# One decoder layer with a grouped mixture of experts: the final combine moved into the expert blocks

## The chip, the cores and the metric

The program runs on one NeuronCore of a Trainium2 chip. The metric is the device time of one execution in microseconds (us). Five engines work side by side, each through its own instructions in order: PE (TensorE, matmuls), DVE (VectorE), ACT (ScalarE), POOL (GpSimd) and SP (SyncE, which only issues DMAs). They meet at semaphores: an instruction raises one when it is done, and another engine waits for a value of it. A DMA raises its semaphore by 16 when it has landed.

## The reference, cut to what matters

The input is a residual stream x of 2048 tokens by 1024, in float32. One layer is computed: a recurrent token mixer, then a mixture of experts, then a last RMS norm.

```python
x = x + g1 * mixer(modulate(rmsnorm(x, norm1_g), sh1, sc1))
hn = modulate(rmsnorm(x, norm2_g), sh2, sc2)
# router: softmax over 16 experts in 4 groups of 4; the best group is chosen,
# and in it the two best experts, with gates that sum to 1
out = sum over the two experts e: (silu(hn @ w_gate[e]) * (hn @ w_up[e]) * gate[e]) @ w_down[e]
x = x + g2 * out
return rmsnorm(x, final_norm_g)
```

The kernel computes each token only for its two experts. Both are of the same group, which the change relies on.

## The kernel before, in words

The stages follow each other, each a block with a barrier behind it: `norm_and_transpose` and `lru` (the mixer), `out_and_norm` (the mixer's output product, the residual sum x2, the second norm and the router's logits), `dispatch`, `experts` and `combine`.

**Tiles.** A token tile has 128 tokens (one per partition); there are NT = 16. `out_and_norm` keeps the 16 tiles of x2 in SBUF for the rest of the program and writes the normed rows hn2 to DRAM.

**Dispatch.** Every (token, expert) pair gets a slot. Slots are sorted by expert, and each expert's slots are filled up to full blocks of 128; at most MAXB = 48 blocks, of which 39 are used with these inputs. Tables in SBUF hold, for each block, the expert, the token of each slot (`slot_token`), the gate of each slot (`slot_gate`), and where weights have to be prepared (`split0`, `split1`). `tab["pos"]` holds for each token its two slots. DVE works these tables out; SP meanwhile fills the unused blocks of the slot buffer `yslot` in DRAM (10 stores, L995).

**Experts.** Products are done in three passes, with each operand as a high and a low part (`w_hi`, `w_lo`, `e_xh`, `e_xl`, `e_ah`, `e_al`). For block b the steps are:

- POOL, `gather(b)`: copies the block's column of token numbers (L1226) and starts an indirect DMA of 128 rows of hn2 into `xg` (L1229). There is one `xg`, so it waits until PE has turned the block before.
- PE, `turn(b)`: transposes `xg`. ACT `high_x`, DVE `low_x`: copy and subtract. PE, `gate_up(b)`: 24 matmuls. ACT `tanh`, DVE `act_product`; PE `turn_act(b)` inside the next block's `gate_up`; ACT `high_a`, DVE `low_a`; PE `down(b)`: 12 matmuls into `pd`.
- DVE, `y_scaled(b)`: `ysb = pd * slot_gate * g2row` (L1327). ACT, `store(b)`: writes `ysb` to its block of yslot (L1277). There is one `ysb`, so the next `y_scaled` waits until the store has landed.

In one turn of its loop each engine works on different blocks: PE does gate_up(i+2), turn(i+3), down(i+1); DVE low_a(i+1), act_product(i+2), low_x(i+3), y_scaled(i+1), low_w(i+2); POOL gather(i+3), low_w(i+1). The order within an engine is as written.

**Weights.** The weights of an expert are four quarters of 128x1536. SP loads them into two raw buffers (quarters 0 and 2, 1 and 3); ACT `high_w` copies a quarter to `w_hi` (L1272); `low_w` subtracts it for `w_lo` (L1214), DVE the even ones and POOL the odd ones. The next expert's quarters 0 and 1 are made in the first block of an expert, 2 and 3 in its second; if it has one block alone, all in that. In further blocks there are none. `low_w` reads per block from the tables whether a piece is due, and if so expert and buffer, into registers.

**Combine.** For each of the 16 token tiles POOL gathers the rows of the token's two slots from yslot (L1446 index copy, L1451 two indirect DMAs), DVE adds them (L1483), adds them to x2 (L1485), ACT squares and sums (L1473) and takes the root (L1475), DVE takes the reciprocal (L1489) and scales by it and by the gain (L1493), SP stores the output tile. Four buffers.

## Time and profile before

| | us |
|---|---|
| three runs: median (lowest to highest) | 1336.73 (1335.91 to 1336.91) |
| the profiled execution | 1335.74 |
| its span, first to last instruction | 1334.2 |
| PE, DVE, ACT, POOL busy | 1082.2, 769.5, 567.3, 563.5 |
| moved by DMA | 207.59 MB, mean 156 GB/s |

The span is the time between the first and the last instruction of the profiled execution; its own time is a little longer. Busy time is the sum of the durations of an engine's instructions, without waits and without the issue of DMAs by other engines than POOL. A share over the whole span is a mean over stages with different limits, so the rows further down are cut by stage.

### The profile page before, as it was taken

Reading aid. Unit: us, or ns where it says so; the run is one execution under the profiler, and the core shown is the slowest. Engines: PE = TensorE matmul, PEld = TensorE weight load, DVE = VectorE, ACT = ScalarE, POOL = GpSimd, SP = SyncE. Lnnn points to the kernel's source line nnn. Section 1 sums busy time; section 2 is a strip of 40 time slices with the busy share of each in tenths; the row PEclk is TensorE's granted clock in tenths of the full one; section 3 lists DMA queues with packets and bytes.
Section 4 is the critical chain, followed back from the end, with each engine's and each line's share of the span. In section 5 each row is a group of like instructions: output and inputs, shape, how many; then the busy total and the mean of one; then the engine's idle time right before and its main releaser. Section 6 shows DMA issues by size and latency. Waiting matters only on the chain. (4 is left out here: it accounts for less than half of the span.)

```text
span 1334.2 us, 19676 instructions
## 1 busy us (share of the span) xinstructions
PE 1082.2 (81%) x4894; PEld 866.6 (65%) x4895; DVE 769.5 (58%) x874; ACT 567.3 (43%) x792; POOL 563.5 (42%) x394
## 2 busy tenths in 40 slices
PE   1459999999999994899999814899999999989300
PEld 0247778778778773688888714677777776767200
DVE  6984676667667664545343376354544545445288
ACT  1554666766776673422222220333433334334033
POOL 0686625525526420145455243333433333334273
PEclk9999999999999997899999855999999999999755
DMA  8544314313313201833324144466756567667498
GB/s 303 175 89 151 99 33 130 84 46 114 93 53 114 63 16 38 311 126 98 139 94 141 48 142 174 135 210 209 262 199 228 189 211 241 206 207 236 145 350 324
DMA packets 126572, 207.59 MB, mean 156 GB/s; under 512 B 16961, under 2 KB 84545, under 8 KB 126417
## 3 DMA queue, kind: packets, MB, share of 16 engines
q1 hardware_dynamic: 106096, 132.81, 30.7%
q0 software_dynamic: 14832, 54.01, 12.0%
q10 hardware_dynamic: 5616, 20.45, 3.8%
q8 instruction: 12, 0.20, 0.1%
q14 instruction: 16, 0.12, 0.0%
HBM read 156.36 MB, written 50.87 MB: 155 GB/s over the span
## 5 line engine op out<-in xcount | busy, mean ns | idle before, releaser
L1214 POOL TENSOR_TENSOR w_lo<-w_raw,w_hi 128x1536 f32 x30 | 107.1, 3570 | 157.8 <-ACT w_hi L1272 157.8
L1377 PE MATMUL e_gu<-w_hi,e_xh 128*128 x312 | 130.2, 417 | 13.7 <-issue 5.0
L1272 ACT ACTIVATE w_hi<-w_raw 128x1536 f32 x60 | 88.3, 1486 | 121.1 <-PE e_pd L1402 46.3
L849 PE MATMUL po<-wo_hi,b_yh 128*128 128x512 f32 x256 | 102.9, 402 | 25.6 <-DVE wo_lo L779 25.6
L1379 PE MATMUL e_gu<-w_hi,e_xl 128*128 x312 | 123.5, 396 | 0.0
L1378 PE MATMUL e_gu<-w_lo,e_xh 128*128 x312 | 122.8, 394 | 0.0
L823 POOL TENSOR_TENSOR x<-x,b_xr 128x1024 f32 (+1 forms) x15 | 49.1, 3273 | 171.9 <-DVE x L787 171.9
L531 DVE SCALAR_TENSOR_TENSOR XB<-xu,conv_w,XB 128x512 f32<-128x512 f32 x96 | 92.6, 965 | 42.2 <-ACT XB L401 38.5
L624 PE MATMUL px<-hT_hi,wx_hi 128*128 128x512 f32 x256 | 101.7, 397 | 5.1 <-DVE wx_lo L465 5.1
L624 PE MATMUL pg<-hT_hi,wg_hi 128*128 128x512 f32 x256 | 104.2, 407 | 0.0
L625 PE MATMUL px<-hT_lo,wx_hi 128*128 128x512 f32 x256 | 101.6, 397 | 0.0
L626 PE MATMUL px<-hT_hi,wx_lo 128*128 128x512 f32 x256 | 101.4, 396 | 0.0
L626 PE MATMUL pg<-hT_hi,wg_lo 128*128 128x512 f32 x256 | 101.1, 395 | 0.0
L625 PE MATMUL pg<-hT_lo,wg_hi 128*128 128x512 f32 x256 | 101.1, 395 | 0.0
L850 PE MATMUL po<-wo_lo,b_yh 128*128 128x512 f32 x256 | 100.4, 392 | 0.0
L851 PE MATMUL po<-wo_hi,b_yl 128*128 128x512 f32 x256 | 100.4, 392 | 0.0
L1327 DVE SCALAR_TENSOR_TENSOR e_y<-e_pd,t_slot_gate,g2row 128x1024 f32<-128x1024 f32 x39 | 50.1, 1284 | 66.2 <-DMA yslot_scratch<-e_y 37.8
L606 POOL TENSOR_TENSOR macc<-macc,mtmp 128x512 f32<-128x512 f32 x56 | 84.4, 1507 | 4.7
L1377 PEld LDWEIGHTS e_gu<-w_hi,e_xh 128*128 128x128 f32 x312 | 59.3, 190 | 39.7 <-issue 29.9
L787 DVE TENSOR_TENSOR x<-po,g1row 128x1024 f32 (+1 forms) x16 | 19.6, 1224 | 108.7 <-PE po L851 108.7
L600 POOL TENSOR_SCALAR macc<-stg,cond 128x512 f32<-128x512 f32 x8 | 12.1, 1512 | 155.2 <-PE pmod L647 151.3
L1400 PE MATMUL e_pd<-w_hi,e_ah 128*128 x156 | 64.8, 415 | 12.1 <-issue 6.5
(260 smaller groups left out, 2639.4 us busy)
## 6 DMA issues: line engine op xcount, KB each, us to landing
yslot_scratch<-e_y ACTq DMA_DIRECT2D x39, 512.0 KB
stg<-in_ada_w_dram POOLq DMA_DIRECT2D x32, 512.0 KB, 4.2
w_raw<-in_moe_w_gate_dram SPq DMA_DIRECT2D x32, 384.0 KB, 3.3
w_raw<-in_moe_w_up_dram SPq DMA_DIRECT2D x32, 384.0 KB, 4.0
n_ada<-in_ada_w_dram SPq DMA_DIRECT2D x16, 512.0 KB, 4.8
n_x<-in_x_dram SPq DMA_DIRECT2D x16, 512.0 KB, 3.4
y_scratch<-M SPq DMA_DIRECT2D x16, 512.0 KB, 3.0
b_yt<-y_scratch SPq DMA_DIRECT2D x16, 512.0 KB, 5.3
```

The costliest lines, as they stand in the source:

```text
L531: nc.vector.scalar_tensor_tensor(xb, xu[:, n, w:w + NB], cw[:, ds(j, 1), w], xb, ALU.mult, ALU.add).then_inc(done, 1)
L624: nc.tensor.matmul(dst[:], whi[br][:, k], hT_hi[:, k, cols], start=(k == 0), stop=False)
L625: nc.tensor.matmul(dst[:], whi[br][:, k], hT_lo[:, k, cols], start=False, stop=False)
L626: last = nc.tensor.matmul(dst[:], wlo[br][:, k], hT_hi[:, k, cols], start=False, stop=(k == KD - 1))
L849: nc.tensor.matmul(po[u][:, cols], yh[u][:, tok], wo_hi[:, k, cols], start=(k == 0), stop=False)
L850: nc.tensor.matmul(po[u][:, cols], yh[u][:, tok], wo_lo[:, k, cols], start=False, stop=False)
L851: last = nc.tensor.matmul(po[u][:, cols], yl[u][:, tok], wo_hi[:, k, cols], start=False, stop=(k == KD - 1))
L1214: tensor_tensor(w["lo"][:, ds(off + q * QW, QW)], w["raw"][:, q % 2], w["hi"][:, ds(off + q * QW, QW)].bitcast(F32), ALU.subtract).then_in ...
L1272: nc.scalar.activation(w["hi"][:, ds(off + q * QW, QW)], w["raw"][:, q % 2], ACT.Copy).then_inc(w["hi_done"], 1)
L1377: nc.tensor.matmul(gu[:], xh[:, tok], hi, start=(k == 0), stop=False)
L1378: nc.tensor.matmul(gu[:], xh[:, tok], lo, start=False, stop=False)
L1379: last = nc.tensor.matmul(gu[:], xl[:, tok], hi, start=False, stop=(k == KD - 1))
```

## The change

The stage `combine`, the slot buffer yslot, its fills and the resident x2 go. Instead:

- `out_and_norm` stores each tile of x2 to DRAM (`x2_dram`), on SP, between the load and the store of hn2.
- Experts are processed in the order 0, 4, 8, 12, 1, 5, ... (`expert_at`): the first experts of the four groups, then the second ones, and so on. The two experts of a token lie at least four experts apart in that order. DVE writes the mask and the positions in this order; SP's loop over experts is written out.
- Each slot gets a code that says whether it is the token's first or second slot. DVE makes three tables of row numbers from it: `row` (the token), `row_first` (the token where the slot is its first, otherwise a number out of range) and `row_second` (likewise for the second). Indirect DMAs skip rows out of range.
- The gate is now multiplied in `act_product`. For each block, POOL gathers the rows of x2 into `xa` (`gather_x`); DVE adds `ysb` to them in `ab` (`accumulate`); POOL scatters `ab` back to x2_dram where it was the first slot (`scatter_acc`); ACT squares and sums `ab` (`square`); POOL works out the reciprocal root by a power and one Newton step, five instructions (`root`); DVE scales to `ob` (`normed`); POOL scatters `ob` to the output where it was the second slot (`scatter_out`). `ysb`, `xa`, `ab` and `ob` are single buffers.

The first and the last turns of the loops are written out in the same manner. The core of the diff:

```diff
-def out_and_norm(nc, sem, cst, io, x2, y_dram, mod_dram, hn2_dram, g2row, logits):
+def out_and_norm(nc, sem, cst, io, y_dram, mod_dram, hn2_dram, x2_dram, g2row, logits):
...
+            def store_x2(it, u):
+                sp.wait_ge(resid, it + 1)
...
+                if at_least(it, 2):
+                    sp.wait_ge(x2_stored[u], it * 8 - u * 8)
...
+                sp.dma_start(x2_dram[ds(it * P, P), :], x2[:, ds(it, 1)].rearrange("p o n -> p (o n)"))\
+                    .then_inc(x2_stored[u], 16)
...
-            pipelined(sp, NT, 6, [(load, 0), (store, 4)])
+            pipelined(sp, NT, 6, [(load, 0), (store_x2, 3), (store, 4)])
...
+def expert_at(i):
+
+    return i % G * PER + i // G
...
@@ dispatch
-            sp.wait_ge(ends_ready, 1)
...
-            with sp.Fori(used, MAXB + 1) as b:
-                sp.dma_start(yslot_dram[ds(b * P, P), :], g2row[:]).then_inc(filled, 16)
...
+            for c in range(TOPK):
+                done(v.tensor_tensor(later[:, c], posf[:, c], posf[:, 1 - c], ALU.is_gt))
+            v.scalar_tensor_tensor(tok2[:], later[:].rearrange("p c t -> p (c t)"), float(SECOND), tok2[:],
+                                   ALU.mult, ALU.add).then_inc(code_ready, 1)
...
-            done(v.tensor_copy(tab["slot_token"][:], pslot[:, 0:MAXB]))
+            done(v.tensor_copy(sci[:], pslot[:, 0:MAXB]))
+            done(v.tensor_scalar(skip1[:], sci[:], float(SECOND), None, ALU.is_gt))
+            done(v.scalar_tensor_tensor(sci[:], skip1[:], -float(SECOND), sci[:], ALU.mult, ALU.add))
+            done(v.tensor_scalar(skip2[:], sci[:], 0.0, float(SKIP), ALU.is_equal, ALU.mult))
+            done(v.tensor_scalar(sci[:], sci[:], -1.0, None, ALU.add))
+            done(v.tensor_tensor(sci[:], sci[:], skip2[:], ALU.add))
+            done(v.tensor_copy(tab["row"][:], sci[:]))
+            done(v.scalar_tensor_tensor(skip2[:], skip1[:], float(SKIP), sci[:], ALU.mult, ALU.add))
+            done(v.tensor_copy(tab["row_first"][:], skip2[:]))
+            done(v.tensor_scalar(skip1[:], skip1[:], -float(SKIP), float(SKIP), ALU.mult, ALU.add))
+            done(v.tensor_tensor(skip1[:], skip1[:], sci[:], ALU.add))
+            done(v.tensor_copy(tab["row_second"][:], skip1[:]))
...
@@ experts, POOL
+            def gather_x(b, first=False):
+                if not first:
+                    pool.wait_ge(xa_in, b * 16)
+                    pool.wait_ge(acc_ready, b)
...
+                nc.gpsimd.tensor_copy(idx_x[:], tab["row"][:, ds(b, 1)]).then_inc(idx_x_ready, 1)
+                pool.wait_ge(idx_x_ready, b + 1)
...
+                pool.indirect_dma_start(xa[:], None, x2_dram, rows(idx_x), **bound).then_inc(xa_in, 16)
+
+            def scatter_acc(b, first=False):
+                if not first:
+                    pool.wait_ge(acc_out, b * 16)
...
+                nc.gpsimd.tensor_copy(idx_a[:], tab["row_first"][:, ds(b, 1)]).then_inc(idx_a_ready, 1)
+                pool.wait_ge(idx_a_ready, b + 1)
+                pool.wait_ge(acc_ready, b + 1)
...
+                pool.indirect_dma_start(x2_dram, rows(idx_a), ab[:], None, **bound).then_inc(acc_out, 16)
+
+            def scatter_out(b, first=False):
+                if not first:
+                    pool.wait_ge(out_done, b * 16)
...
+                nc.gpsimd.tensor_copy(idx_o[:], tab["row_second"][:, ds(b, 1)]).then_inc(idx_o_ready, 1)
+                pool.wait_ge(idx_o_ready, b + 1)
+                pool.wait_ge(out_ready, b + 1)
...
+                pool.indirect_dma_start(out[0], rows(idx_o), ob[:], None, **bound).then_inc(out_done, 16)
+
+            def root(b, first=False):
+
+                pool.wait_ge(squared, b + 1)
...
+                nc.gpsimd.tensor_scalar(var[:], ssq[:], 1.0 / D, EPS, ALU.mult, ALU.add).then_inc(rstd_step, 1)
...
+                nc.gpsimd.tensor_tensor(root0[:], var[:], nhalf[:], ALU.pow).then_inc(rstd_step, 1)
...
+                nc.gpsimd.tensor_tensor(part[:], root0[:], root0[:], ALU.mult).then_inc(rstd_step, 1)
...
+                nc.gpsimd.tensor_scalar(part[:], part[:], var[:], -0.5, ALU.mult, ALU.mult).then_inc(rstd_step, 1)
...
+                if not first:
+                    pool.wait_ge(out_ready, b)
...
+                nc.gpsimd.tensor_scalar(rstd[:], part[:], 1.5, root0[:], ALU.add, ALU.mult).then_inc(rstd_ready, 1)
+
+            nc.gpsimd.memset(xg[:], 0.0).then_inc(cleared, 1)
+            nc.gpsimd.memset(xa[:], 0.0).then_inc(cleared, 1)
+            nc.gpsimd.memset(nhalf[:], -0.5).then_inc(cleared, 1)
...
-            with pool.Fori(0, nless) as i:
+            with pool.Fori(3, nless) as i:
                 gather(i + LEAD)
                 low_w(pool, nc.gpsimd.tensor_tensor, i + 1, 1)
+                scatter_acc(i - 1)
+                gather_x(i)
+                root(i - 1)
+                scatter_out(i - 2)
...
@@ experts, ACT
+            def square(b, first=False):
+                act.wait_ge(acc_ready, b + 1)
+                if not first:
+                    act.wait_ge(rstd_ready, b)
...
+                nc.scalar.activation(squares[:], ab[:], ACT.Square, accum_out=ssq[:]).then_inc(squared, 1)
...
+            with act.Fori(2, nless) as i:
+                square(i - 1)
                 high_a(i + 1)
                 tanh(i + 2)
-                store(i)
                 high_x(i + 3)
                 high_w(i + 2)
...
@@ experts, DVE
-                nc.vector.scalar_tensor_tensor(ysb[:], pd[:], tab["slot_gate"][:, ds(b, 1)], g2row[:],
-                                               ALU.mult, ALU.mult).then_inc(y_ready, 1)
+                nc.vector.tensor_tensor(ysb[:], pd[:], g2row[:], ALU.mult).then_inc(y_ready, 1)
+
+            def accumulate(b, first=False):
+                dve.wait_ge(y_ready, b + 1)
+                dve.wait_ge(xa_in, (b + 1) * 16)
+                if not first:
+                    dve.wait_ge(squared, b)
+                    dve.wait_ge(out_ready, b)
+                    dve.wait_ge(acc_out, b * 16)
+                nc.vector.tensor_tensor(ab[:], ysb[:], xa[:], ALU.add).then_inc(acc_ready, 1)
+
+            def normed(b, first=False):
+                dve.wait_ge(rstd_ready, b + 1)
+                if first:
+                    dve.wait_ge(fg_in, 16)
+                else:
+                    dve.wait_ge(out_done, b * 16)
...
+                nc.vector.scalar_tensor_tensor(ob[:], ab[:], rstd[:], fg[:], ALU.mult, ALU.mult).then_inc(out_ready, 1)
...
+            with dve.Fori(2, nless) as i:
                 low_a(i + 1)
                 act_product(i + 2)
                 low_x(i + 3)
                 dues = [per_block(dve, f"split{part}", i + 2, 0, 1) for part in range(2)]
+                normed(i - 1)
+                accumulate(i)
                 y_scaled(i + 1)
                 low_w(dve, nc.vector.tensor_tensor, i + 2, 0, dues)
...
-def combine(nc, sem, cst, io, tab, x2, yslot_dram, out):
...
```

## Rows read from the trace of the kernel before

**Rows 1.** Windows by stage; columns: five engines busy us (count), clock, DMA share, GB/s.

```profile
0.00:120.00 120.00, 57.20 (x204) 41.10 (x206) 91.82 (x113) 49.85 (x84) 66.75 (x38) 1.00 0.60 190
...
780.00:828.00 48.00, 17.60 (x68) 15.36 (x68) 40.83 (x78) 3.70 (x3) 24.31 (x21) 0.50 0.47 175
828.00:1252.00 424.00, 386.50 (x1794) 302.76 (x1794) 200.88 (x264) 157.45 (x216) 151.18 (x108) 0.98 0.61 203
1252.00:1334.00 82.00, 0.00 (x0) 0.00 (x0) 60.57 (x65) 24.40 (x49) 45.00 (x48) 0.51 0.85 320
```

**Rows 2.** The page's chain that ended last, by engine and line.

```profile
DVE f_ya L1483 1%; DVE x L1485 1%; DMA f_yb<-yslot_scratch,f_idx 1%; POOL f_yb L1451 0%; POOL f_ya L1451 0%; DVE f_ob L1493 0%; POOL f_idx L1446 0%; DVE f_rstd L1489 0%; ACT f_junk L1473 0%; DVEq L1485 0%; DVEq L1492 0%; DVEq L1484 0%; ACT f_std L1475 0%; DVEq L48 0%; DVEq L1493 0%
```

**Rows 3.** Groups by form, 800 to 1334 us: xcount, busy us, mean ns, idle.

```profile
L1493 DVE SCALAR_TENSOR_TENSOR f_ob<-x,f_rstd,f_g 128x1024 f32<-128x1024 f32 x16 | 20.5, 1284 | 2.1 <-DVE f_rstd L1489 0.8
L1483 DVE TENSOR_TENSOR f_ya<-f_ya,f_yb 128x1024 f32<-128x1024 f32 x16 | 19.6, 1222 | 14.2 <-DMA f_yb<-yslot_scratch,f_idx 14.2
```

**Rows 4.** Timeline of DVE: start us, length us, instruction, idle before.

```profile
856.76 1.28 DVE L1327 SCALAR_TENSOR_TENSOR e_y<-e_pd,t_slot_gate,g2row 128x1024 f32<-128x1024 f32 x1 [1.31 <-PE e_pd L1402]
...
1251.31 1.28 DVE L1327 SCALAR_TENSOR_TENSOR e_y<-e_pd,t_slot_gate,g2row 128x1024 f32<-128x1024 f32 x1 [3.45 <-PE e_pd L1402]
```

**Rows 5.** Waits of POOL, 828 to 1256 us; us in total, times, longest.

```profile
POOL w_lo L1214 <- ACT w_hi L1272: 157.8, 30, 9.0
POOL e_idx L1226 <- PE e_tp L1359: 66.2, 10, 7.8
```

**Rows 6.** Timeline of all engines where the expert stage starts.

```profile
826.28 0.21 DVE L1143 TENSOR_SCALAR t_slot_gate<-pslot 128x48 f32<-128x48 f32 x1
...
874.03 1.09 ACT L1253 ACTIVATE e_xh<-e_tp 128x512 fp32r<-128x512 f32 x2 [0.49 <-PE e_tp L1359]
...
880.61 3.79 POOL L1214 TENSOR_TENSOR w_lo<-w_raw,w_hi 128x1536 f32 x1 [4.46 <-ACT w_hi L1272]
```

**Rows 7.** Groups of POOL by form, whole span.

```profile
L951 POOL MEMSET keep<- 128x256 f32 x1 | 0.3, 313 | 0.0
```

**Rows 8.** Timeline of POOL at the start of the combine.

```profile
1261.19 0.94 POOL L1451 DMA_INDIRECT f_yb<-yslot_scratch,f_idx  x1 [0.30 <-issue]
1262.14 0.19 POOL L1446 COPY f_idx<-t_pos 128x2 int32<-128x2 int32 x1
1263.10 0.96 POOL L1451 DMA_INDIRECT f_ya<-yslot_scratch,f_idx  x1 [0.77 <-POOL f_idx L1446]
```

**Rows 9.** Groups by form, 828 to 1252 us.

```profile
L1214 POOL TENSOR_TENSOR w_lo<-w_raw,w_hi 128x1536 f32 x30 | 107.1, 3570 | 157.8 <-ACT w_hi L1272 157.8
```

**Rows 10.** Tile e_xg; durations ns min/median/max, and its landing.

```profile
L1229 POOL DMA_INDIRECT e_xg<-hn_scratch,e_idx x39: 961/983/1084, 828.9 to 1224.8; - x39
...
DMA to landing us min/median/max: 4.2/5.3/7.6
```

**Rows 11.** Timeline: ACT stores e_y, and the next e_y of DVE.

```profile
1190.30 0.34 ACTq L1277 DMA_DIRECT2D yslot_scratch<-e_y  x1
...
1193.96 1.28 DVE L1327 SCALAR_TENSOR_TENSOR e_y<-e_pd,t_slot_gate,g2row 128x1024 f32<-128x1024 f32 x1 [1.08 <-DMA yslot_scratch<-e_y]
```

**Rows 12.** Timeline of ACT before a weight copy.

```profile
1200.91 1.09 ACT L1253 ACTIVATE e_xh<-e_tp 128x512 fp32r<-128x512 f32 x2 [0.49 <-PE e_tp L1359]
1205.03 1.49 ACT L1272 ACTIVATE w_hi<-w_raw 128x1536 f32 x1 [3.03 <-issue]
```

**Rows 13.** Timeline of POOL later in the combine, DVE adding beside it.

```profile
1281.19 0.90 POOL L1446 COPY f_idx<-t_pos 128x2 int32 x1
1282.87 1.41 POOL L1451 DMA_INDIRECT f_ya<-yslot_scratch,f_idx  x1 [0.77 <-POOL f_idx L1446]
```

**Rows 14.** Timeline of POOL in the block with two pieces.

```profile
1179.56 3.68 POOL L1214 TENSOR_TENSOR w_lo<-w_raw,w_hi 128x1536 f32 x1 [4.18 <-ACT w_hi L1272]
1189.38 3.52 POOL L1214 TENSOR_TENSOR w_lo<-w_raw,w_hi 128x1536 f32 x1 [6.13 <-ACT w_hi L1272]
```

**Rows 15.** Windows around PE's longest stand in the expert stage.

```profile
1180.00:1185.00 5.00, 4.79 (x13) 3.38 (x14) 0.00 (x0) 0.31 (x1) 3.24 (x1) 0.66 0.61 181
```

More of the change, by code:

```diff
@@ L1161, in _, with experts @@
                                  start=(it == 0), stop=(it == N - 1)).then_inc(slotted, 1)
-def experts(nc, sem, cst, io, tab, w, hn2_dram, yslot_dram, g2row):
+def experts(nc, sem, cst, io, tab, w, hn2_dram, x2_dram, g2row, out):
     ctx = ExitStack()
@@ L1198, in _ @@
                 load_quarter(sp, io, w, 1, q)
-            with sp.Fori(2, E) as e:
+            sp.dma_start(fg[:], io["final_norm_g"].partition_broadcast(P)).then_inc(fg_in, 16)
+            for e in range(2, E):
                 for q in range(NQ):
@@ L1337, in _ @@
             low_w(dve, nc.vector.tensor_tensor, 1, 0)
-            with dve.Fori(0, nless) as i:
+            low_a(1)
+            act_product(2)
+            low_x(3)
+            accumulate(0, True)
+            y_scaled(1)
+            low_w(dve, nc.vector.tensor_tensor, 2, 0)
+            low_a(2)
+            act_product(3)
+            low_x(4)
+            normed(0, True)
+            accumulate(1)
+            y_scaled(2)
+            low_w(dve, nc.vector.tensor_tensor, 3, 0)
+            with dve.Fori(2, nless) as i:
                 low_a(i + 1)
@@ L1346, in _ @@
             act_product(nless + 2)
+            normed(nless - 1)
+            accumulate(nless)
             y_scaled(nless + 1)
@@ L1349, in _ @@
             low_a(nless + 2)
+            normed(nless)
+            accumulate(nless + 1)
             y_scaled(nless + 2)
+            normed(nless + 1)
+            accumulate(nless + 2, )
+            normed(nless + 2)
         @block.tensor
@@ L1541, in build @@
                  "hi_done": sem("w_hi_done"), "lo_done": [sem("w_lo_done0"), sem("w_lo_done1")]}
[L1542 to L1544 removed]
+            dispatch(nc, sem, cst, io, logits, tab, w)
+            experts(nc, sem, cst, io, tab, w, hn2_dram, x2_dram, g2row, out)
 _INS = ["x", "c", "ada_w", "ada_b", "norm1_g", "norm2_g", "lru_w_in", "lru_conv_w", "lru_conv_b", "lru_wa", "lru_ba",
```

220 lines of the change are left out of this document (110 added, 110 removed).

## The prediction

> **What bounds the kernel now.** I read the windows by stage first, then the chain of waits, then the waits of POOL. From 828 to 1252 us runs the expert stage: PE is busy for 386.5 of 424 us at a clock of 0.98, so PE bounds it, while POOL is busy for 151 us only. From 1252 to 1334 runs the combine: PE does nothing, DVE is busy for 60.6 of 82 us [rows 1]. The chain that ended last names the three large DVE operations of the combine and its gathers [rows 2]; two of them last 1.22 and 1.28 us [rows 3]. So 82 us can be won. What they are bought with is the period of the expert stage: the scaled outputs of blocks 0 and 38 start at 856.76 and 1251.31 [rows 4], 394.5 us for 38 blocks, 10.4 us each. There are 39 blocks. 29 of them carry weight splitting on POOL (30 pieces, two in one block); the other 10 don't. Before these pieces POOL waits 157.8 us for ACT, and 66.2 us for PE's turns in the 10 blocks without [rows 5]. POOL's 151 busy us hide its pauses, which matters below.
>
> **Start of the stage.** After the last product DVE does 13 small operations where it did 2, at 0.21 us like the last one there [rows 6]: +2.3. POOL clears two tiles of 128x1024 and a column before its first gather; a memset of a quarter of the size takes 0.31 [rows 7], so I take 2.3 for all (bounds 0.6 and 2.6). The stage starts 4.6 us later. The removed fills on SP, three removed casts, the stores of x2 in the stage before (16 of them on SP, waiting for a sum that is ready before the hn2 row that SP stores next) and the gain row on SP are taken at nothing: another engine's work ends each stage. They cost 2 us if that cover is gone.
>
> **POOL's work for one block.** Before: one indirect DMA. After: four (gather of hn2, gather of x2, scatter of the sum, scatter of the output), each with its own index copy, and five small operations for the root. In the combine a copy of 0.19 starts as soon as a DMA ends, a pause of 0.77 and the next DMA of 0.96 follow, and a second DMA comes 0.30 after a first [rows 8]: with the expert stage's 0.98 for the DMA [rows 10], 1.94 us per indirect transfer, and the engine does nothing else in the pause, since it runs in order. Four are 7.76. The root: five operations of 0.19 (the index copy's duration) and four handovers on the same engine. Below stand 0.08 (1.27 in all), above 0.47, which is the pause of 0.77 less the 0.30 that a DMA takes anyway (with a fifth, 3.3 in all); I take 0.2, so 1.75, as the pause is that of an instruction that DMA issue follows, not arithmetic. A weight piece is 3.5 [rows 9]. A block with a piece therefore holds POOL for 7.76 + 1.75 + 3.5 = 13.0 us, one without for 9.5. The first is already over the 10.4 of PE.
>
> **The loop across the engines.** The tiles ab, xa and ob are single. DVE's normed(b) waits until scatter_out(b-1) has landed; accumulate(b+1) stands behind it on DVE, and scatter_acc(b+1) waits for that; on POOL gather_x(b+2), root(b+1) and then scatter_out(b) follow, which the next normed waits for. One turn of this loop yields one block: normed 1.28 + 0.06, accumulate 1.22 [rows 3], handover 0.1; the scatter's DMA, whose index is already copied, 0.30 + 0.98; gather_x 1.94; root 1.75; copy and pause of scatter_out 0.96; its landing L; handover 0.1. For L the gathers show 4.2 at least and 5.3 as median [rows 10]; ACT's store to DRAM, issued at 1190.30, releases DVE at 1193.96, 3.7 later [rows 11]. A scatter whose rows out of range are skipped moves half the bytes, but stands behind gather_x in the same queue: I take 4.4, bounds 3.7 and 5.3. Sum 13.1 us (bounds 11.7 and 15.5). So even a block without a weight piece takes 13.1, and POOL's gather and piece lie in the landing.
>
> The Trainium skill (DMA: Bandwidth & Descriptors, "Anatomy of one DMA — SWDGE (gpsimd) path") fits a transfer by 2.0 us plus bytes over 436 GB/s. By it a 512 KB gather takes 3.2, and the trace disagrees (4.2 at least). With 2.6 for the half-filled scatter, the loop would be 11.3, the blocks with a piece would still be set by POOL's sum, and the time would be 18 us less.
>
> **What is added in a block with a piece.** Two costs have no row on POOL. First its register reads: with two branches and five reads ACT starts a weight copy 3.03 us after the end of the copies before it, for "issue" alone [rows 12]; POOL has three or four reads, and 0.98 of DMA to hide them, so 0 to 1.7. Second, POOL against DVE: while DVE adds tiles from SBUF in the combine, an index copy takes 0.90 for 0.20 and a DMA 1.41 for 0.96 [rows 13]. Normed and accumulate, 2.5 us of such work, fall into POOL's piece after the change: 0 to 1.6. I take 1.3 for both together: 14.3 us (bounds 12.5 and 17.7).
>
> The Trainium skill (GPSIMD Engine Reference, "Key points") says that the two engines share their SBUF interface and collide when a DVE instruction has two SBUF inputs. The trace agrees; taken to the full it gives the upper 1.6 in each of 26 such blocks, 42 us in all.
>
> **The sum.** Block 4 is turned at 874.03 [rows 6]; plus 4.6, 878.6. POOL: gather(5) to 880.6; the piece that began at 880.61 begins at 885.2 and ends at 888.9; scatter_acc(1), gather_x(2), root(1) and the copy of scatter_out(0) take 1.94 + 1.94 + 1.75 + 0.96, to 895.5; landing and handover to 900.0; normed(1) and accumulate(2) end at 902.6. From accumulate(2) to accumulate(38) are 36 periods. The pieces of blocks 4 to 38 lie in them: 27, as 3 came earlier. The split of tokens over experts is the same, only their order changes, so one block still has both: the second piece began 6.13 after the end of the first, waiting for the weights [rows 14], +6.1 + 3.5. That makes 25 x 14.3 = 357.5, one of 23.9, and 10 x 13.1 = 131: 512.4. After accumulate(38): square 1.3, root 1.75, normed 1.4, the last scatter 0.4 + 4.4: 9.3. Span 902.6 + 512.4 + 9.3 = 1424. The profiled execution took 1335.74 for a span of 1334.2, so 1.5 outside, and the median of the three runs lies 1.0 above it: **1427 us**, 6.7% slower. What the combine gives back (82) is over-paid by 36 periods of 14.2 on average instead of 10.4 (138); the later start, the first turns of the loop and the tail are the other 34. With the low bounds everywhere the periods are 25 x 12.5 + 22.1 + 10 x 11.7 = 451.6 and the time 1365; with the high ones 1543.
>
> **PE in all this** has 9.9 us of work in some 14. It will stand still for two spells a block, for its turn and for e_al, since ACT's square now comes ahead of high_a. Before, a stand of 4 us took the clock from 2.4 to 1.2 GHz for a while (0.66 over 5 us, so 1.7 us lost) [rows 15]. PE has over 3 us free per block to cover that. It is a term of its own only if the clock stays low throughout: see below.
>
> **Rivals.**
> 1. *It all hides under PE.* The period stays 10.4, the last e_y comes 4.6 later than now, and accumulate and the tail follow: 1251.31 + 4.6 + 1.3 + 1.2 + 9.3 + 2.5 = 1270 us, 5% faster. It needs POOL to hold under 10.4 on average with 0.77 x 3.5 = 2.7 for pieces: (10.4 - 2.7 - 1.3) / 4 = 1.6 us for each indirect transfer, against 1.94, and a loop of 10.4 against 11.7 at least. For it speaks only that POOL is busy for 151 of 424 us now. 5%.
> 2. *POOL bounds, the loop hides.* POOL's sum alone at its low price, 39 x (7.76 + 1.27) + 30 x 3.5 = 457, from 832.4, with 20 for the first turns and the last block's chain and 2.5 around: 1312, 1.8% faster. The point is whether normed finds scatter_out landed; the order on POOL (scatter_out last, right after root) speaks against. 5%; with partial waits it comes out within 0.2% of now, 3%.
> 3. *The clock stays at 1.2 GHz.* PE's 9.9 us become nearly 20, 39 x 9 more than 10.4: some 1640 us. In the first 120 us PE stood still half of the time at full clock [rows 1], which speaks against; from 780 to 828, at 17.6 busy of 48, it ran at 0.50, which speaks for. 3%.
> 4. *My forecast*, 84%, with its upper end (registers, collisions and long landings together, over 1480) at 7 of these; its own range is 1350 to 1480.
>
> **Chances and range.** A measurement of this kernel tells 0.2% (2.7 us) from no change. Faster: rivals 1 and 2, 0.10. Same 0.03. Slower 0.87. I leave out the two faster cases, the slow clock and the top, 0.20 in all, and reach down to no change: 1334 to 1480.
>
> **What the profile after would show.** Right: PE busy for about two thirds of the stage; DVE's longest wait is that of e_ob for the DMA out<-e_ob; POOL with few waits in blocks with a piece; e_ab 13 us apart without a piece, 14 to 15 with; about 1.9 us from index copy to end of each DMA; last e_ab near 1415. Wrong: if PE waits little and e_ab is under 11 us apart (rival 1); if POOL's queue is full and e_ob waits for e_rstd only (rival 2); if the root takes over 3 us, or L is far from 4.4, the size is off and not the loop.

## The result, and the profile after

The changed kernel takes 1557.49 us (median of 4 runs, 1549.85 to 1562.73) against 1336.32 for the kernel before (4 runs, 1334.18 to 1336.91): the ratio is 1.165, 95% interval 1.160 to 1.170. The forecast had the direction and the structure, and was 130 us short of the size. The profiled execution took 1549.85 us for a span of 1548.3; it is the fastest of the four, so its rows tell some 8 us less than the median.

Windows by stage of the changed kernel (length, then busy us of PE, weight load, DVE, ACT and POOL, then clock, DMA share, GB/s) answer to [rows 1]:

```profile
560.00:780.00 220.00, 209.68 (x1067) 176.60 (x1065) 89.36 (x82) 51.23 (x78) 95.80 (x36) 0.95 0.38 136
780.00:838.00 58.00, 17.59 (x68) 15.35 (x68) 49.35 (x106) 6.45 (x6) 26.94 (x26) 0.50 0.25 81
838.00:1543.00 705.00, 453.61 (x1794) 356.20 (x1794) 349.54 (x342) 197.15 (x294) 413.74 (x538) 0.79 0.42 137
```

The combine is gone, 82 us, but the expert stage has grown from 424 to 705. PE has the same 1794 matmuls in it and is busy for 64% of it, at a clock of 0.79 instead of 0.98. Here is one block with a weight piece on POOL, that is, one quarter of an expert's weights that POOL has to subtract (start us, length us, instruction, idle time before it and what ended it):

```profile
905.95 0.20 POOL L1265 COPY e_idx<-t_row 128x1 int32 x1
907.01 1.05 POOL L1268 DMA_INDIRECT e_xg<-hn_scratch,e_idx  x1 [0.85 <-POOL e_idx L1265]
910.14 3.45 POOL L1250 TENSOR_TENSOR w_lo<-w_raw,w_hi 128x1536 f32 x1 [2.09 <-issue]
913.53 1.72 POOL L1284 COPY e_idx_a<-t_row_first 128x1 int32 x1
916.18 1.06 POOL L1288 DMA_INDIRECT x_scratch<-e_ab,e_idx_a  x1 [0.93 <-POOL e_idx_a L1284]
917.24 0.19 POOL L1275 COPY e_idx_x<-t_row 128x1 int32 x1
918.29 1.04 POOL L1278 DMA_INDIRECT e_xa<-x_scratch,e_idx_x  x1 [0.86 <-POOL e_idx_x L1275]
919.41 0.19 POOL L1304 TENSOR_SCALAR e_var<-e_ssq 128x1 f32<-128x1 f32 x1
...
921.49 0.18 POOL L1294 COPY e_idx_o<-t_row_second 128x1 int32 x1
922.58 1.10 POOL L1298 DMA_INDIRECT out_dram<-e_ob,e_idx_o  x1 [0.91 <-POOL e_idx_o L1294]
923.69 0.19 POOL L1265 COPY e_idx<-t_row 128x1 int32 x1
```

From one index copy to the next are 17.7 us, and no pause in between is ended by another engine: POOL waits for its own copies and for "issue" alone (time for which the profile shows no releaser; POOL's register reads stand at this place). It is full, with gaps that are its own. In other blocks the pause before the piece ends with ACT's weight copy, 18 times, and is 1.0 to 4.6 us long but for one of 10.7. The waits of the stage by engine (us, times, longest) answer to [rows 5]:

```profile
DVE e_ob L1487 <- DMA out_dram<-e_ob,e_idx_o: 248.1, 38, 10.6
PE e_pd L1581 <- DVE e_al L1463: 93.3, 25, 9.2
POOL w_lo L1250 <- ACT w_hi L1401: 50.6, 18, 10.7
POOL x_scratch L1288 <- DVE e_ab L1478: 32.9, 9, 5.8
```

What matters is where the engine at the bound waits for others: POOL does so for 104.2 us of 705 (the last two rows, 11.6 for PE, 6.5 for ACT's square and 2.6 for a DMA), where it did for 224 of 424 before. Register reads lie hidden in the 50.6 us for ACT, so the true wait is shorter. DVE's 248.1 us for the landing of the output scatter were forecast as the sign of the loop, but they appear whenever POOL issues that scatter late, whatever made it late. A block without a piece shows the loop itself:

```profile
1511.82 1.09 POOL L1298 DMA_INDIRECT out_dram<-e_ob,e_idx_o  x1 [0.90 <-POOL e_idx_o L1294]
1515.34 1.28 DVE L1487 SCALAR_TENSOR_TENSOR e_ob<-e_ab,e_rstd,e_fg 128x1024 f32<-128x1024 f32 x1 [8.07 <-DMA out_dram<-e_ob,e_idx_o]
1516.83 1.23 DVE L1478 TENSOR_TENSOR e_ab<-e_y,e_xa 128x1024 f32<-128x1024 f32 x1 [0.20 <-DVE e_ob L1487]
1518.89 0.97 POOL L1288 DMA_INDIRECT x_scratch<-e_ab,e_idx_a  x1 [5.77 <-DVE e_ab L1478]
1520.94 1.06 POOL L1278 DMA_INDIRECT e_xa<-x_scratch,e_idx_x  x1 [0.88 <-POOL e_idx_x L1275]
1525.21 1.10 POOL L1298 DMA_INDIRECT out_dram<-e_ob,e_idx_o  x1 [0.90 <-POOL e_idx_o L1294]
```

Here POOL does stand still, 5.77 us for accumulate, and one turn is 1525.21 - 1511.82 = 13.4 us; the forecast said 13.1. POOL waits for accumulate in nine periods, all of them without a piece.

**Collisions.** A DVE operation that reads two tiles from SBUF and a POOL operation that reads SBUF do not share the time, they take turns; the later one starts its work when the earlier one is done. In the first fence POOL's piece runs beside DVE's accumulate, in the second, of the kernel before, POOL splits weights while DVE compares and multiplies 256 elements per partition, which takes 0.42 us when it is alone (a row of that form 4 us later):

```profile
1087.95 3.77 POOL L1250 TENSOR_TENSOR w_lo<-w_raw,w_hi 128x1536 f32 x1 [1.02 <-ACT w_hi L1401]
1088.62 4.18 DVE L1478 TENSOR_TENSOR e_ab<-e_y,e_xa 128x1024 f32<-128x1024 f32 x1 [0.22 <-DVE e_ob L1487]
1091.67 1.17 POOL L1284 COPY e_idx_a<-t_row_first 128x1 int32 x1
```

```profile
788.20 6.98 POOL L968 TENSOR_TENSOR w_lo<-w_raw,w_hi 128x1536 fp32r<-128x1536 f32 x2 [2.94 <-ACT w_hi L1007]
788.78 3.13 DVE L1044 TENSOR_TENSOR chosen<-work,d_m 128x256 f32<-128x256 f32 x1
791.94 3.52 DVE L1045 TENSOR_TENSOR chosen<-chosen,rank_w 128x256 f32<-128x256 f32 x1
```

Accumulate ends 1.1 us after POOL's piece, that is, it begins its work when the piece is done; POOL's next copy, of 0.2 us by itself, then ends with accumulate. The last three rows were in the trace of before and I had not read them.

In the block shown above, the copy of 1.72 us ended with another operation, DVE's own weight piece, which takes 1.76 alone and had waited for POOL's:

```profile
912.31 2.89 DVE L1250 TENSOR_TENSOR w_lo<-w_raw,w_hi 128x1536 f32 x1 [0.74 <-issue]
```

Of the 38 copies of this kind (`e_idx_a`), 14 took 1.7 us and ended with DVE's weight piece, 13 took 1.2 and ended with accumulate, four were held a little by normed, and 7 took 0.2. The forecast had counted normed and accumulate alone.

### The profile page after: what moved, and what is told of

Read it like the earlier page. It is cut to its first block and busy times, and to the rows that moved or that the text cites. A ratio compares the mean times of both kernels' runs of the same rounds, so it can differ in the third digit from the quotient of the medians.

```text
span 1548.3 us, 20709 instructions
## 1 busy us (share of the span) xinstructions
PE 1153.3 (74%) x4894; PEld 920.5 (59%) x4895; DVE 859.9 (56%) x900; ACT 582.1 (38%) x821; POOL 780.4 (50%) x776
## 3 DMA queue, kind: packets, MB, share of 16 engines
q0 software_dynamic: 26928, 67.15, 13.4%
## 5 line engine op out<-in xcount | busy, mean ns | idle before, releaser
L1487 DVE SCALAR_TENSOR_TENSOR e_ob<-e_ab,e_rstd,e_fg 128x1024 f32<-128x1024 f32 x39 | 50.1, 1284 | 248.1 <-DMA out_dram<-e_ob,e_idx_o 248.1
L1581 PE MATMUL e_pd<-w_hi,e_ah 128*128 x156 | 87.7, 562 | 104.9 <-DVE e_al L1463 93.3
L1250 POOL TENSOR_TENSOR w_lo<-w_raw,w_hi 128x1536 f32 x30 | 114.2, 3808 | 68.3 <-ACT w_hi L1401 50.6
L1401 ACT ACTIVATE w_hi<-w_raw 128x1536 f32 x60 | 87.7, 1484 | 159.4 <-DMA w_raw<-in_moe_w_down_dram 108.4
L1558 PE MATMUL e_gu<-w_hi,e_xh 128*128 x312 | 131.6, 422 | 13.1 <-DVE w_lo L1250 9.7
L1409 ACT ACTIVATE e_sq<-e_ab 128x1024 f32<-128x1024 f32 x39 | 41.3, 1059 | 248.0 <-DVE e_ab L1478 248.0
L1559 PE MATMUL e_gu<-w_lo,e_xh 128*128 x312 | 126.6, 406 | 0.0
L1581 PEld LDWEIGHTS e_pd<-w_hi,e_ah 128*128 128x128 f32 x156 | 41.8, 268 | 121.7 <-issue 112.9
L626 PE MATMUL pg<-hT_hi,wg_hi 128*128 128x512 f32 x256 | 104.2, 407 | 0.0
L602 POOL TENSOR_SCALAR macc<-stg,cond 128x512 f32<-128x512 f32 x8 | 11.6, 1446 | 156.1 <-PE pmod L649 151.7
L1478 DVE TENSOR_TENSOR e_ab<-e_y,e_xa 128x1024 f32<-128x1024 f32 x39 | 84.6, 2169 | 8.4 <-DVE e_ob L1487 8.4
```

Source lines behind the costliest of these rows:

```text
L626: nc.tensor.matmul(dst[:], whi[br][:, k], hT_hi[:, k, cols], start=(k == 0), stop=False)
L1250: tensor_tensor(w["lo"][:, ds(off + q * QW, QW)], w["raw"][:, q % 2], w["hi"][:, ds(off + q * QW, QW)].bitcast(F32), ALU.subtract).then_in ...
L1401: nc.scalar.activation(w["hi"][:, ds(off + q * QW, QW)], w["raw"][:, q % 2], ACT.Copy).then_inc(w["hi_done"], 1)
L1478: nc.vector.tensor_tensor(ab[:], ysb[:], xa[:], ALU.add).then_inc(acc_ready, 1)
L1558: nc.tensor.matmul(gu[:], xh[:, tok], hi, start=(k == 0), stop=False)
L1559: nc.tensor.matmul(gu[:], xh[:, tok], lo, start=False, stop=False)
```

## The experiments

Times are medians; ratios are to the kernel before in the same session, with 95% intervals. The last two columns give the mean period from one scatter of a sum to the next, for blocks with one piece on POOL and without; the block with two pieces is left out.

```
kernel                      us      ratio [interval]        with a piece   without
changed                   1557.5   1.165 [1.160, 1.170]      18.2           13.7
out scatter early         1518.9   1.139 [1.136, 1.142]      17.7           12.4
register reads early      1560.3   1.170 [1.168, 1.173]      17.7           14.6
short root                1541.4   1.155 [1.153, 1.158]      17.5           14.0
no collision              1480.2   1.110 [1.107, 1.114]      16.1           12.0
pieces on DVE             1476.4   1.106 [1.104, 1.109]      -              15.1
light POOL                1387.9   1.040 [1.037, 1.042]      -              12.9
 + two pairs of copies    1390.4   1.040 [1.038, 1.043]      -              13.1
 + x2 stores unheld       1389.9   1.040 [1.038, 1.043]      -              13.0
 + four raw buffers       1367.2   1.024 [1.021, 1.026]      -              12.3
changed, four raw buffers 1557.9   1.166 [1.163, 1.170]      18.2           13.5
short root, four raw      1537.6   1.153 [1.150, 1.155]      17.6           13.9
 + out scatter early      1462.0   1.095 [1.092, 1.098]      16.4           10.7
before + x2 stores        1347.9   1.009 [1.006, 1.011]
before + interleaving     1330.4   0.996 [0.994, 0.997]
```

**1. The output scatter early.**

```diff
                 gather(i + LEAD)
+                scatter_out(i - 2)
                 low_w(pool, nc.gpsimd.tensor_tensor, i + 1, 1)
                 scatter_acc(i - 1)
                 gather_x(i)
                 root(i - 1)
-                scatter_out(i - 2)
```

> Edit: in every turn of POOL's loop scatter_out(i-2) stands right behind gather(i+3), ahead of the weight piece, and no longer last. POOL's work is the same; the output scatter lands long before the next normed. Theory A (POOL is the bound by the sum of its own work, 17.6 us in a block with a piece and 12.4 in one without; DVE's 248 us of waiting for the output scatter are only the time until POOL comes to it): the time stays at 1545 to 1570 us, DVE's wait moves to e_rstd. Theory B (the loop normed, accumulate, scatter, gather, root, scatter_out and its landing is the bound, as forecast): the loop loses the landing and the scatter's 1.1 us, 3 us or more per block, 39 x 3: some 1440 us.

Measured 1518.9, 38 us less. The landing has left the loop: normed now waits 201.3 us for the root and not for the DMA. Yet a block with a piece still takes 17.7 us. The landing was not what bound it; POOL's work was. That work stayed the same only in its sum: the piece and the copy behind it are now undisturbed, but normed holds the first index copy, accumulate the first DMA and DVE's weight piece the output DMA, 2.9 us in all:

```profile
1085.38 1.25 POOL L1265 COPY e_idx<-t_row 128x1 int32 x1 [0.28 <-issue]
1087.53 1.52 POOL L1268 DMA_INDIRECT e_xg<-hn_scratch,e_idx  x1 [0.89 <-POOL e_idx L1265]
1090.18 2.37 POOL L1298 DMA_INDIRECT out_dram<-e_ob,e_idx_o  x1 [0.93 <-POOL e_idx_o L1294]
```

**2. The register reads of the two branches ahead of the gather.**

```diff
             with pool.Fori(3, nless) as i:
+                dues = [per_block(pool, f"split{h}", i + 1, 0, 1) for h in range(2)]
                 gather(i + LEAD)
-                low_w(pool, nc.gpsimd.tensor_tensor, i + 1, 1)
+                low_w(pool, nc.gpsimd.tensor_tensor, i + 1, 1, dues)
```

> Edit: POOL reads the two flags for a weight piece ahead of gather(i+3) instead of between it and the piece, where a pause of 2.0 us (with a piece) and 0.7 us (without) stands that the profile puts down to issue. Theory A: the pause is POOL's own and counts in full; two of four reads go under the DMA before, 0.5 to 1 us less in 26 blocks and 0.7 in 9: 1520 to 1545 us. Theory B: POOL's pauses lie in the landing, no change (1550 to 1563).

A miss: 1560.3, no gain. The profile says why. The "issue" pause before w_lo fell from 17.7 to 2.8 us in all, and one of 17.1 appeared before the index copy: nothing hides the reads there. Blocks with a piece gained 0.5 us (18.2 to 17.7), those without lost 0.9 (13.7 to 14.6), and the 36 periods of the trace took 617.7 us instead of 621.1.

**3. The root in two operations**, one power without the correction after it (this changes the last digits of the result).

```diff
-                nc.gpsimd.tensor_tensor(root0[:], var[:], nhalf[:], ALU.pow).then_inc(rstd_step, 1)
-                ...
-                nc.gpsimd.tensor_scalar(rstd[:], part[:], 1.5, root0[:], ALU.add, ALU.mult).then_inc(rstd_ready, 1)
+                nc.gpsimd.tensor_tensor(rstd[:], var[:], nhalf[:], ALU.pow).then_inc(rstd_ready, 1)
```

> Edit: root without the Newton step, two POOL operations instead of five (the output differs in its last digits only). The five take 2.1 us in the trace, the two would take 0.95. Theory A and theory B both have root on the path in every block: 39 x 1.15 = 45 us less, 1505 to 1520 us. If the time stays, neither is right.

16 us less instead of 45. POOL's waits for ACT's copies rose from 50.6 to 70.3, those for accumulate from 32.9 to 47.5, 34 us together. Something stands close behind POOL's sum; experiments 9 and 10 look for it.

**4. No collision.** In the loop DVE's piece, accumulate and normed run on 16 columns; the rest of these results is left out.

```diff
-                normed(i - 1)
-                accumulate(i)
+                normed(i - 1, few=16)
+                accumulate(i, few=16)
```

> Edit: in the loop DVE does its weight piece, accumulate and normed on 16 columns only (the rest of these three results is left out); all waits and all of POOL's work stay. Theory A with collisions: POOL's copy of the scatter index falls from 1.7 to 0.2 us, its weight piece from 3.8 to 3.5, and nothing else: 26 x 1.8 + 9 x 1.0 = 56 us less, about 1500. Theory A without collisions being of weight: 1545 to 1560. Theory B: the loop also loses 2.3 us of normed and accumulate and the 3 us by which e_ab is stretched in 12 blocks: 39 x 2.3 + 12 x 3 = 125 us less, 1430.

1480.2, 77 us less, nearer to the forecast with collisions than to that of the loop. Here the turn-taking is laid bare: DVE's operation on 16 columns, 0.17 us by itself, takes 2.90, to the end of POOL's:

```profile
1012.75 3.43 POOL L1250 TENSOR_TENSOR w_lo<-w_raw,w_hi 128x1536 f32 x1 [0.98 <-issue]
1013.32 2.90 DVE L1250 TENSOR_TENSOR w_lo<-w_raw,w_hi 128x16 f32 x1 [0.53 <-issue]
1016.13 0.18 POOL L1284 COPY e_idx_a<-t_row_first 128x1 int32 x1
```

POOL's operations by group, in the changed kernel and in this one (busy us, mean ns):

```profile
L1250 POOL TENSOR_TENSOR w_lo<-w_raw,w_hi 128x1536 f32 x30 | 114.2, 3808 | 68.3 <-ACT w_hi L1401 50.6 <-issue 17.7
L1284 POOL COPY e_idx_a<-t_row_first 128x1 int32 x36 | 40.7, 1129 | 7.6 <-issue 7.6
L1275 POOL COPY e_idx_x<-t_row 128x1 int32 x36 | 16.9, 469 | 0.3
```

```profile
L1250 POOL TENSOR_TENSOR w_lo<-w_raw,w_hi 128x1536 f32 x30 | 103.8, 3460 | 66.4 <-ACT w_hi L1401 35.9 <-issue 30.5
L1284 POOL COPY e_idx_a<-t_row_first 128x1 int32 x36 | 6.5, 180 | 7.5 <-issue 7.5
L1275 POOL COPY e_idx_x<-t_row 128x1 int32 x36 | 6.9, 190 | 0.3
```

10.4 + 34.2 + 10.0, and 3.2 of the gathers of x2, make 58 us that collisions took from POOL (its gathers of hn2 and its scatters changed by 0.1 us). The other 19 us or so are not settled by this run: it also takes DVE's own 2.1 us out of each turn of the loop.

**5. All pieces on DVE.**

```diff
+            if odd:
+                return
...
-                    q = 2 * part + odd
-                    eng.wait_ge(w["hi_done"], NQ * e + (q + 1))
+                    for q in (2 * part, 2 * part + 1):
+                        eng.wait_ge(w["hi_done"], NQ * e + (q + 1))
```

> Every odd quarter of the weight splitting goes from POOL to DVE, which then does all four quarters of an expert; POOL's order of transfers and root is unchanged. If POOL's own serial work sets the period, a block with a piece loses the piece, the pause before it and the collisions with it (17.9 to about 12.4 us) and all blocks look alike: 26 x 5.4 = 140 us less, about 1400 to 1420. If the loop across the engines sets it (normed, accumulate, scatter, gather_x, root, scatter_out, landing), it was hidden beside the piece and the blocks stay above 15 us: 1500 or more. If the collision alone is the cause, 2 to 3 us per block with a piece go: about 1480.

1476.4, below the 1500 of the loop and above the 1400 to 1420 of POOL's sum, close to the 1480 given for collisions alone, though POOL's piece went as well. With POOL relieved the loop comes to the front in nearly every block, as the waits from 840 to 1370 us show, and with DVE's doubled pieces it takes 15.1 us on average, 12.3 to 13.7 where there is no piece:

```profile
DVE e_ob L1489 <- DMA out_dram<-e_ob,e_idx_o: 134.0, 30, 6.0
ACT e_sq L1411 <- DVE e_ab L1480: 127.4, 30, 13.3
POOL x_scratch L1290 <- DVE e_ab L1480: 104.6, 30, 4.9
```

So the forecast's loop is real and stands 3 us behind POOL's sum. "All blocks look alike at 12.4" was wrong: I had left out that very loop.

**6. A light POOL**: the edits of 1, 3 and 5 together.

> Three changes together: all weight splitting on DVE, the scatter of the output rows right behind the first gather, and the inverse root in two operations instead of five (one power without the correction step; it changes the last digits). POOL is left with four indirect transfers of 2.1 us and a root of 1.0: 9.4 to 9.8 us per block, less than the 10.4 of PE before. If POOL's sum is the bound, the period falls to 10.4 to 11.5 us in every block and the time to 1290 to 1340. If the loop across the engines is the bound once POOL is light, the period stays at 12 to 13 us: 1390 to 1420.

1387.9: 170 us less, 2 us below the range of the second theory; the mean period is 12.9, as it said. The savings are worth more together (170) than alone (38 + 16 + 81 = 135), which fits two bounds close together: each saving alone meets the other.

**7. Two pairs of index copies, and gather_x ahead of the scatter of the sum.**

```diff
+                index(i)
                 gather(i + LEAD, copied=True)
                 scatter_out(i - 2, copied=True)
+                index_x(i)
+                gather_x(i, copied=True)
                 scatter_acc(i - 1, copied=True)
-                gather_x(i)
                 root(i - 1)
```

> On top of the light POOL order (all splitting on DVE, output scatter early, root in two operations): the index copies stand in two pairs per block, so that two of the four pauses of 0.9 between a copy and its DMA shrink to 0.3; and gather_x goes ahead of scatter_acc (the blocks that share a token are at least four apart), which shortens the way from one accumulate to the next by one scatter, 2.1 us. In the light order 22 of 36 periods were 12.3 us or longer while POOL's own sum was 9.8. If the way accumulate, scatter, gather_x, landing, accumulate set them, the period falls by some 1.5 to 2 us in the blocks of 12.5 and the time to 1325 to 1350. If DVE (8.9 us of work and its pauses, now with all pieces) sets them, it stays at 1375 to 1388.

A miss: 1390.4, nothing gained, though the second DMA of a pair does come 0.30 after the first. The edit brought a wait of its own: the scatter of the sum is now issued later, and accumulate, which needs `ab` free, waits for its landing instead of that of the gather. The first row is of experiment 6, the second of this one, both of the whole expert stage:

```profile
DVE e_ab L1472 <- DMA e_xa<-x_scratch,e_idx_x: 35.8, 19, 3.2
DVE e_ab L1491 <- DMA x_scratch<-e_ab,e_idx_a: 38.8, 12, 4.4
```

In one stretch successive blocks now take 11.6 to 12.2 and 16.1 to 17.0 us in turn, and ACT stands in the long ones:

```profile
1064.16 1.49 ACT L1414 ACTIVATE w_hi<-w_raw 128x1536 f32 x1 [4.94 <-DMA w_raw<-in_moe_w_down_dram]
```

**8. The same without SP's wait for the x2 store two tiles back** (see 11), **and then with four raw weight buffers** instead of two, so that ACT need not wait.

```diff
-    raw, arrived = w["raw"][:, q % 2, :], w["in"][q]
+    raw, arrived = w["raw"][:, q, :], w["in"][q]
...
-                    sp.wait_ge(w["lo_done"][q % 2], 2 * e + q // 2)
+                    sp.wait_ge(w["lo_done"][q % 2], 2 * e - 1 + q // 2)
```

> On top of the previous kernel (light POOL, two pairs of copies, free x2 stores): four raw weight buffers instead of two, so that a quarter is loaded as soon as the same quarter of the expert before is split, and ACT does not wait for it. In that kernel periods alternate between 11.1 and 17 us where each of two successive blocks carries half an expert's weights, and ACT waits 89.9 us for the loads with the squares queued behind it. If this chain of buffers (copy, split, load, copy) sets the long blocks, they fall to 11 to 12 us and the time to 1320 to 1345. If POOL or the collisions with DVE's splitting set them, it stays over 1375.

1367.2, 23 us less, between the two: the chain of the buffers was a part of it. The long blocks of that stretch still take 16.

**9. The changed kernel with four raw buffers and nothing else, and with the short root.** The edits are those of 8 and 3.

> The changed kernel with four raw weight buffers instead of two, nothing else. If POOL's own serial work sets the blocks with a piece, nothing is gained by earlier loads: within 10 us of 1557. If the chain of the buffers (ACT waits 108 us for the loads) is as long as POOL's sum, which would explain why the savings of the register reads and of the root were given back, 30 to 60 us go.

> The changed kernel with the root in two operations and four raw weight buffers. Each alone: 16 us less, and nothing. If the chain of the two raw buffers stands close behind POOL's sum and took back what the short root saved, the two together give the full saving of 39 x 1.1 = 43 us: about 1515. If something else took it back, it stays at 1535 to 1545.

1557.9: no gain, though ACT's wait of 108.4 us for these loads is gone, and blocks with a piece take 18.2 us as before. That is the clearest word for POOL's sum in these blocks. Only the block with two pieces gained in the trace, 29.9 to 22.2 us; the output stage before it ended 10 us later there (see 11), which hides that in the total. And 1537.6 with the short root: the buffers did not take its saving back. POOL's wait for accumulate is now 55.4 us in 14 blocks, against 32.9 in 9.

**10. The same with the output scatter early.**

(The order of experiment 1 on top of the short root and the four buffers.)

> The previous kernel with the output scatter right behind the first gather (alone 38 us less). If POOL's sum sets the period and the buffers are out of the way, the savings add up: 1515 - 38, about 1475 to 1480. If collisions between POOL and DVE grow when the order is denser, or another chain takes over, it stays over 1495.

1462.0: 96 us below the changed kernel, where the parts alone gave 38, 16 and 0, and lower than the forecast for POOL's sum. With the landing out of the loop POOL doesn't wait for accumulate any more, and the short root and the buffers give 57 us on top of experiment 1, against 20 without it. That fits the loop as what had taken the root's saving back; root and buffers were not tried apart here.

**11. The x2 stores.** First the kernel before with the stores of the changed one, which nothing reads; then, on top of experiment 7, without the wait:

```diff
-                if at_least(it, 2):
-                    sp.wait_ge(x2_stored[u], it * 8 - u * 8)
                 sp.dma_start(x2_dram[ds(it * P, P), :], x2[:, ds(it, 1)].rearrange("p o n -> p (o n)"))\
```

> The kernel before with one addition: SP stores each tile of x2 to DRAM in the output projection, as the changed kernel does, and nothing reads it. The forecast priced this at nothing. If these 8 MB are what delays that stage (its end comes 6.7 us later in the trace of the changed kernel), the time rises by 5 to 7 us: 1339 to 1342. If something else delays it, the time stays within 0.2% of before.

> The previous kernel, and SP no longer waits for the landing of the store of x2 two tiles earlier before it issues the next one; it waits for all of them at the end of the stage. If it was this wait on SP that held up the loads and the hn2 stores queued behind it (the output stage ends 6.7 us later in the changed kernel, and the stores alone cost 11.8 us in the kernel before), 6 to 10 us go. If it is the traffic itself, 8 MB in a stage that moved 23 MB, nothing goes. With both steps it could come within 1% of the kernel before, on either side.

The stores cost 11.8 us, more than forecast by either. Without SP's wait nothing comes back (1389.9 against 1390.4), so it is not that wait. ACT waits for the store of hn2 two tiles back; the first row is of the kernel before, the second with x2 stores, both from 560 to 780 us:

```profile
ACT b_hn L750 <- DMA hn_scratch<-b_hn: 114.0, 12, 9.8
```

```profile
ACT b_hn L761 <- DMA hn_scratch<-b_hn: 125.0, 12, 11.0
```

The hn2 stores' median landing goes from 4.6 to 5.2 us. That speaks for the traffic, but it is not the only thing that moved. SP issues one more DMA per tile, between the load of x and the store of hn2, so that this store is issued later behind the load (the first two rows are of the kernel before):

```profile
659.67 0.33 SPq L717 DMA_DIRECT2D b_xr<-in_x_dram  x1
660.28 0.35 SPq L728 DMA_DIRECT2D hn_scratch<-b_hn  x1
```

```profile
664.11 0.35 SPq L718 DMA_DIRECT2D b_xr<-in_x_dram  x1
664.96 0.36 SPq L733 DMA_DIRECT2D x_scratch<-x  x1
665.53 0.35 SPq L738 DMA_DIRECT2D hn_scratch<-b_hn  x1
```

Over the first 12 tiles the median distance goes from 0.59 to 1.20 us, and is 1.09 without SP's wait. The cost is 11.8 / 16 = 0.74 per tile, and either 0.6 could be most of it. A run with the x2 stores on another engine would tell the two apart; it wasn't made.

**12. The kernel before with the interleaving alone.**

```diff
-            v.tensor_tensor(mask, oh1, oh2, ALU.add).then_inc(mask_ready, 1)
+            v.tensor_tensor(placed_as(mask), at(oh1), at(oh2), ALU.add).then_inc(mask_ready, 1)
```

> The kernel before with the interleaving of the experts by group alone (order of slots, order in which the weights are loaded, SP's loop over experts written out). The forecast priced this at nothing: the same 39 blocks and 30 pieces, only in another order. Both theories of the loss (POOL's sum, the loop across the engines) say within 0.2% of before. If the order matters (where the blocks without a piece lie, and so how the loads of the weights are spread), it is off by 5 us or more.

1330.4, 0.45% faster (0.3 to 0.6): small, but clear of the noise, and the only version here that beats both kernels. Its last e_y starts at 1243.01 instead of 1251.31 [rows 4]. Why this order suits the loads better I did not take apart.

## Why the prediction was wrong

- **Direction, combine, path.** Right: the combine's 82 us are over-paid by the expert stage, PE is busy for two thirds of it (64%), and rivals 1 and 2 (it all hides, 1270; POOL bounds cheaply, 1312) did not come. That the blocks with a piece are set by POOL's own sum was the forecast's own statement.
- **The step that failed: "I take 1.3 for both together: 14.3 us".** The 1.3 stood for the register reads and the collisions in a block with a piece. The 25 periods with one piece took 18.2 us on average, 3.9 more each, 98 us of the 124 by which the span of the profiled execution missed. This term is 2.9 us of it, the rest the transfers and the root. By groups, POOL's sum is now: four indirect transfers 8.5 (forecast 7.76: the DMA takes 1.05 to 1.1 and the pause 0.9, not 0.98 and 0.77), root 2.2 (1.75: the power alone takes 0.57), the piece 3.5 without a collision, as forecast, the pause before it 2.3 (68.3 us over 30; register reads, 1.0 to 2.1 where they stand alone, and behind them ACT's copy), collisions 1.9 (58 us over 30, an estimate from experiment 4). Together 18.4. The last two are 4.2 where 1.3 stood. I had given both bounds (1.7 and 1.6) and then took less than half of their sum; the upper bound of the block, 17.7, would have been 0.5 short (its own terms add up to 17.9). The bound of the collision was too low for two reasons. I had left out DVE's own weight piece, which ends the long copies of 1.7. And I read it from [rows 13], where the other engine's operation is 1.2 us long; beside a piece of 3.5 accumulate takes up to 4.5 instead of 1.22, though it is DVE that loses there.
- **The loop.** Near: 13.4 measured in undisturbed turns, 13.7 on average over the ten blocks without a piece (12.4 to 16.5), 13.1 forecast. That it came so near is in part luck, as its parts were off and cancel: L with its handover is 3.5 from the issue of the DMA (1511.82 to 1515.34), not 4.5, while the way from accumulate to its scatter is 0.8 and not 0.4, the root is 0.4 longer, gather_x 0.2, normed and the last pause 0.1 each. The low bound of 11.7 is 0.2 lower than its terms give.
- **The double block.** 29.9, forecast 23.9. Its second piece waited 10.7 us for ACT's copy, where 6.1 had been read from before; ACT in turn waited for the load. With four raw buffers the block takes 22.2 (experiment 9).
- **The start.** accumulate(2) ended at 910.2, forecast 902.6. "The stores of x2 ... are taken at nothing" failed: they delay the output stage by 6.7 us in this trace, by up to 17 in those of the experiments, and cost 11.8 alone. The dispatch and the memsets (0.95 each) were near.
- **The tail.** 17.0 after the last accumulate, forecast 9.3: normed(38) waits for the landing of the scatter before it, which the sum had left out, and the last landing takes 5.7.
- **The clock.** 0.79 over the stage; the same 1794 matmuls keep PE busy for 453.6 us instead of 386.5. PE has room for that, in line with the forecast, and rival 3 did not come. No run held the clock up, so that it costs nothing is read from POOL's sum, not shown.
- **The range.** 1480 stood for "registers, collisions and long landings together" at a chance of 7 in 100. The first two were not rare events but present in every block with a piece; long landings were not needed.

The Trainium skill (SBUF — State Buffer, "SBUF: two separate sides") calls the port pair that VectorE and GpSimd share an exclusive lock: who starts first keeps it for the whole instruction, and a VectorE operation with two SBUF inputs takes part in this against a GpSimd operation that reads SBUF. The traces agree: 2.90 us for 0.17. They agree on the condition too: y_scaled, with one of its two inputs in PSUM, takes 1224 to 1226 ns in all 39 blocks, pieces beside it or not. In the forecast I had drawn on a milder sentence and sized it from a 1.2 us neighbour; by this rule the collision of one pair would have been up to a whole piece.

**Still open:** the split of the 77 us of experiment 4 between collisions and loop; how much of the pause before a piece is register reads and how much ACT; whether the x2 stores cost by their traffic or by SP's issue; what keeps the light versions at 11 to 16 us (DVE's splitting now blocks POOL's copies and DMAs, up to 2.6 us for one of 1.05, but this was not tried apart); and the gain by the order of the experts.

## What to carry to other kernels

When an engine of many small steps comes to carry a stage, add up its whole line, pauses and register reads included, and where an operation of POOL that reads SBUF can fall beside one of DVE with two inputs in SBUF, price it at up to the full length of the neighbour, not a share of it. Moving an operation on POOL moves the collision rather than removing it, as experiment 1 shows. A saving on the bound is worth only the distance to the next loop, so look for the pair of changes that moves both. The longest wait in a trace names a follower; in this case the bound was the engine whose idle time hardly anybody else ended.

## What the runs showed of the hardware

- DVE with two inputs in SBUF against POOL reading SBUF: whole instructions exclude each other (2.90 us for a 16-column operation of 0.17; a copy of 0.18 took 1.13 on average, up to 1.72). POOL's issue of an indirect DMA is held too: 2.37 instead of 1.02 us beside DVE's weight piece. With one input in PSUM DVE is not held (1.22 us, 39 times).
- An indirect DMA of 128 rows of 4 KB holds POOL for 0.97 to 1.10 us when nothing collides. Behind a copy on POOL it starts after 0.9 us; with its indices ready, 0.30 after the DMA before it.
- The output scatter, which skips rows, released its tile 3.4 to 3.5 us after its issue in the turns shown; over all 39 blocks it landed after 2.2 to 5.7, 3.3 at the median; the gathers of x2 after 3.2 to 7.4 us, 5.7 at the median.
- The pause before a piece on POOL that no other engine ends, where its register reads for two branches and an offset stand, is 1.0 to 2.1 us, and 0.7 before the copy in a block without a piece. Behind the DMA issues of 2.4 to 2.6 us of experiment 1, 0 to 0.35 us are left of it.
- 16 stores of 512 KB added on SP to a stage at a DMA share of 0.31 cost 11.8 us; the landing of the other stores went from 4.6 to 5.2 us and their issue came 0.6 later.
